# Attention tiles of a hybrid decoder layer: tail sums ahead of the fox logits, the fox V column as a unit of its own tile, TensorE's tiles unrolled

## The reference, cut to the token mixer

```python
def stick_breaking_block(q_blk, k_pre, v_pre, q_start):
    z = einsum('bhqd,bhkd->bhqk', q_blk, k_pre) * HEAD_DIM ** -0.5
    causal = s_idx < t_idx
    log_1m_beta = where(causal, log_sigmoid(-z), 0.0)
    tail = cumsum(log_1m_beta, axis=3, reverse=True) - log_1m_beta
    a = where(causal, exp(log_sigmoid(z) + tail), 0.0)
    return einsum('bhqk,bhkd->bhqd', a, v_pre)

def forgetting_block(q_blk, k_pre, v_pre, fcum_q, fcum_k, q_start):
    logits = einsum('bhqd,bhkd->bhqk', q_blk, k_pre) * HEAD_DIM ** -0.5
    logits = logits + fcum_q[..., :, None] - fcum_k[..., None, :]
    logits = where(s_idx <= t_idx, logits, -inf)
    return einsum('bhqk,bhkd->bhqd', softmax(logits, axis=-1), v_pre)

def token_mixer(h, w_in, b_forget, sb_group_g, fox_group_g, w_out):
    proj = h @ w_in        # q_sb k_sb v_sb q_fx k_fx v_fx (512 columns each), 8 forget logits
    fcum = cumsum(log_sigmoid(f_logit + b_forget))
    merged = concat(rms_norm(o_sb, sb_group_g), rms_norm(o_fx, fox_group_g))
    return merged @ w_out
```

## Time and profile before

| | us |
|---|---|
| three runs: median (lowest to highest) | 1053.41 (1053.15 to 1053.46) |
| the profiled execution's own time | 1053.56 |
| its span, first to last instruction | 1051.7 |
| mixer, PE's first product to the end of the last tile | 358.6 to 599.3 of the span |

### The profile page before, as it was taken

One profiled execution on the slowest core, in us unless ns is written; L12 is line 12 of the kernel. 1 busy time (PEld: TensorE's weight loads), 2 busy tenths in 40 slices (PEclk: granted clock), 3 DMA queues, 4 the chain that ended last, 5 costly groups with the idle time before them and its releaser, 6 DMA issues.

```text
span 1051.7 us, 16615 instructions
## 1 busy us (share of the span) xinstructions
PE 1038.6 (99%) x6118; PEld 923.7 (88%) x6118; DVE 785.5 (75%) x1107; ACT 558.4 (53%) x922; POOL 10.0 (1%) x33
## 2 busy tenths in 40 slices
PE   9999999999999999999999999999999999999997
PEld 7889999998888878888888888889999998888886
DVE  6889888864343789796969889899888865454655
ACT  6634444343333558686869846544444344344645
POOL 1000000000002000000000000000000000000000
PEclk9999999999999999999999999999999999999999
DMA  6353423303323233232312122263423305444002
GB/s 213 94 175 106 135 81 106 98 21 111 95 94 100 61 100 90 62 88 58 85 51 61 56 85 81 83 188 108 134 81 105 97 21 162 144 135 159 1 21 80
DMA packets 99948, 100.59 MB, mean 96 GB/s; under 512 B 6672, under 2 KB 82192, under 8 KB 99888
## 3 DMA queue, kind: packets, MB, share of 16 engines
q1 hardware_dynamic: 99472, 99.47, 31.2%
q10 hardware_dynamic: 416, 0.30, 0.1%
HBM read 94.44 MB, written 2.10 MB: 92 GB/s over the span
## 4 chain that ended last, share of the span: by engine, by line
PE 87%; DVE 6%; ACT 4%; issue 2%; DMA 0%; DVEq 0%; ACTq 0%
PE bank L1758 27%; PE bank L1759 27%; PE bank L1760 27%; PE bank L2100 2%; DVE w_r L1110 1%; PE bank L2115 1%; DVE scratch L1656 1%; ACT scratch L847 0%; DVE big L1436 0%; DVE big L1453 0%; PE bank L2064 0%; ACT scratch L845 0%; DVE big L1433 0%; DMA gains<-in_gains 0%; DVE acc L1130 0%
## 5 line engine op out<-in xcount | busy, mean ns | idle before, releaser
L1110 DVE TENSOR_TENSOR w_r<-w_raw,w_r 128x512 fp32r<-128x512 f32 x204 | 138.0, 688 | 134.2 <-ACT w_r L611 128.6
L1758 PE MATMUL bank<-big,w_r 128*128 128x512 f32 (+1 forms) x676 | 236.1, 349 | 0.1
L1759 PE MATMUL bank<-big,w_r 128*128 128x512 f32 (+1 forms) x676 | 235.1, 348 | 0.0
L1760 PE MATMUL bank<-big,w_r 128*128 128x512 f32 (+1 forms) x676 | 235.0, 348 | 0.0
L611 ACT ACTIVATE w_r<-w_raw 128x512 fp32r<-128x512 f32 x204 | 125.3, 627 | 182.4 <-PE bank L1760 179.1
L1758 PE MATMUL bank<-big,xg 128*128 128x256 f32 (+1 forms) x728 | 214.2, 294 | 0.0
L1760 PE MATMUL bank<-big,xg 128*128 128x256 f32 (+1 forms) x728 | 213.7, 294 | 0.0
L1759 PE MATMUL bank<-big,xg 128*128 128x256 f32 (+1 forms) x728 | 213.7, 293 | 0.0
L666 ACT ACTIVATE xg<-over 128x1024 fp32r<-128x1024 f32 x72 | 75.4, 1055 | 143.4 <-DVE over L1199 90.0
L1758 PE MATMUL bank<-xg,w_r 128*128 128x512 f32 x378 | 150.1, 397 | 0.6 <-DVE scratch L1427 0.6
L1759 PE MATMUL bank<-xg,w_r 128*128 128x512 f32 x378 | 147.4, 390 | 0.0
(11 more groups left out here) (204 smaller groups left out, 1270.1 us busy)
## 6 DMA issues: line engine op xcount, KB each, us to landing
w_raw<-in_ffn_w_down SPq DMA_DIRECT2D x88, 256.0 KB, 2.7
over<-in_ffn_w_gate SPq DMA_DIRECT2D x24, 512.0 KB, 4.1
over<-in_ffn_w_up SPq DMA_DIRECT2D x24, 512.0 KB, 5.4
w_raw<-in_w_in SPq DMA_DIRECT2D x36, 256.0 KB, 3.1
w_raw<-in_ffn_w_up SPq DMA_DIRECT2D x24, 256.0 KB, 2.8
w_raw<-in_ffn_w_gate SPq DMA_DIRECT2D x23, 256.0 KB, 2.8
w_raw<-in_ffn_w_up SPq DMA_DIRECT2D x8, 512.0 KB, 5.8
w_raw<-in_ffn_w_gate SPq DMA_DIRECT2D x8, 512.0 KB, 6.8
```

What stands on the lines that cost most here:

```text
L1110: dve.tensor_tensor(w_slot(1, slot, 0, 4 * P), w_raw[:, slot, :], plain(w_slot(0, slot, 0, 4 * P)), SUB).then_inc(w_lo, 1)
L1758: pe.matmul(dst, w_hi_ap, m_hi, start=start, stop=False, skip_group_check=True)
L1759: pe.matmul(dst, w_lo_ap, m_hi, start=False, stop=False, skip_group_check=True)
L1760: return pe.matmul(dst, w_hi_ap, m_lo, start=False, stop=stop, skip_group_check=True)
```

## The change

- On PE the tail sums come ahead of the fox logits in every head: `project(0)`, in the first head the transpose of the sb V, the tail sums, `first_logits`, in the first head the transpose of the fox V, `project(1)`, `logits(1)`, and then as before. In the last tile the parts stand where they stood between these, parts(0) ahead of the tail sums.
- On ACT and DVE the softmax of logits 3, 2, 0 comes behind the sb weights, directly ahead of that of logits 1, and the split of the fox V behind both. `weigh(0)` waits as before, the first head's for both V splits.
- `mixer_start` projects five column groups in ten units, sb V in two units of its own (`mix_v`). Fox V is projected by `project(0)` of the tile itself; the other five of a tile are still projected one tile ahead, in the order fox q, fox k, sb q, sb k, sb V. The last tile gets one projection (24 matmuls), in its first head. The number of matmuls stays as it was.
- `qk_split(j + 1, 0)` (sb q and k), which follows logits 1 of the second head, now waits for that head's `project_out(1)`; the fox one waits for a column of the first head.
- The forget gate's matmuls are spread over the chunks; its weights are split at the first chunk, and unit splits between chunks begin at the second chunk; DVE's gate chain stands ahead of the hold of q and k.
- SP's order follows the units; `double_k` and `double_fx` of the last tile stand two parts earlier.
- PE's tiles are unrolled; ACT and DVE keep their loops.

The diff, cut to its core, with eight columns of indentation taken off:

```diff
 U_MIX = U_DOWN[0] + DOWN_UNITS
+U_TILE = U_MIX + TILE_UNITS - 2
...
+MIX_PAIRS = [(3, 4), (0, 1)]
+MIX_FIRST = [(2, 0), (2, 1), None, (3, 0), (3, 1), (0, 1), (0, 0), (1, 1), (1, 0), None]
+MIX_V = [u for u, unit in enumerate(MIX_FIRST) if unit is None]
+MIX_BANK = [0, 1, 7, 4, 6]
+TILE_COLS = [[5, 3, 4], [0, 1, 2]]
...
     w_six = w_in[:, :, 0:6 * 512].rearrange("p k (c n) -> p k c n", n=512)
-    for j, (kp, cp) in enumerate(MIX_FIRST):
+    for j, unit in enumerate(MIX_FIRST):
         u = U_MIX + j
+        if unit is None:
+            kh = 1 - MIX_V.index(j)
+            load_unit(u, u % SLOTS, w_in[:, 4 * kh:4 * kh + 4, 512 * 2:512 * 2 + P], 4)
+            continue
+        kp, cp = unit
...
-    for tile in range(1, TILES):
+    def tile_unit(tile, j):
+        c = TILE_COLS[j // 6][j % 6 // 2]
+        kh = j % 2
+        at = 512 * c + (tile if c == 5 else tile + 1) * P
+        u = U_TILE + TILE_UNITS * tile + j
+        load_unit(u, u % SLOTS, w_in[:, 4 * kh:4 * kh + 4, at:at + P], 4)
+    for tile in range(TILES - 1):
         for j in range(TILE_UNITS):
-            c, kh = divmod(j, 2)
             if j == 5:
-                double_k(tile - 1)
-            if j == (6 if tile == 1 else 5):
-                double_fx(tile - 1)
-            load_unit(U_MIX + TILE_UNITS * tile + j, j % SLOTS,
-                      w_in[:, 4 * kh:4 * kh + 4, 512 * c + tile * P:512 * c + tile * P + P], 4)
+                double_k(tile)
+            if j == (5 if tile else 6):
+                double_fx(tile)
+            tile_unit(tile, j)
+    tile_unit(TILES - 1, 0)
+    tile_unit(TILES - 1, 1)
     w_out = t["w_out"][0].rearrange("(k p) n -> p k n", p=P)
     for r in range(PARTS):
-        if r == 5:
+        if r == 3:
             double_k(TILES - 1)
             double_fx(TILES - 1)
...
         first = isinstance(tile, int) and tile == 0
-        act.wait_ge(hold_ready, (2, 4)[kind] if first else 6 * tile + 3 * kind)
+        act.wait_ge(hold_ready, (2, 4)[kind] if first else 6 * tile + (3, 1)[kind])
...
     def mixer_start():
-        for j in range(EARLY, 9):
-            ahead(U_MIX, 0, TILE_UNITS, j)
...
-        ahead(U_MIX, 0, TILE_UNITS, 9)
         qk_split(0, 1)
...
             if hh == 0:
                 v_split(j, 0)
-                v_split(j, 1)
                 if not more:
+                    ahead(U_TILE, j, TILE_UNITS, 0)
+                    ahead(U_TILE, j, TILE_UNITS, 1)
                     unit(0)
-            for i, b in enumerate((3, 2, 0)):
-                softmax_exp(i, b)
             if hh == 1 and more:
                 unit(0)
                 unit(1)
...
                 act.activation(el[:, c], Z[b][:, 0:Z_W[b]], ACT.Exp).then_inc(a_exp, 1)
                 act.wait_ge(a_exp, 3 * hd + b + 2)
                 act.activation(sp_r[0][:, c], el[:, c], ACT.Copy).then_inc(a_hi, 1)
+            for i, b in enumerate((3, 2, 0)):
...
             softmax_exp(3, 1)
+            if hh == 0:
+                v_split(j, 1)
             if hh == 0 and more:
...
+    def beside_x(k):
+        if k == 0:
+            act.wait_ge(wf_zero, 1)
+            act.wait_ge(wf_loaded, 16)
+            act.activation(wf_part[0], wf_raw, ACT.Copy).then_inc(wf_hi, 1)
+        else:
+            ahead(U_MIX, 0, TILE_UNITS, k - 1)
...
+    def beside_x(k):
+        if k == 0:
+            dve.wait_ge(wf_hi, 1)
+            dve.tensor_tensor(wf_part[1], wf_raw, plain(wf_part[0]), SUB).then_inc(wf_lo, 1)
+        else:
+            ahead(U_MIX, 0, TILE_UNITS, k - 1)
...
-        for j in range(EARLY, 9):
-            ahead(U_MIX, 0, TILE_UNITS, j)
-            if j == EARLY:
-                dve.wait_ge(wf_hi, 1)
-                dve.tensor_tensor(wf_part[1], wf_raw, plain(wf_part[0]), SUB).then_inc(wf_lo, 1)
+        ahead(U_MIX, 0, TILE_UNITS, 7)
         dve.memset(scan_ones, 1.0).then_inc(f_step, 1)
-        dve.wait_ge(rms_ready, SUM_AT[N_MIX_PRE] + 1)
-        dve.memset(acc[:, 0, :], 0.0).then_inc(acc_zero, 1)
-        dve.memset(acc[:, 1, :], 0.0).then_inc(acc_zero, 1)
         def hold_pair(cp):
             dve.wait_ge(w_used, U_MIX + MIX_FIRST.index((ORDER[1][-1] // 2, cp)) + 1)
             for c in MIX_PAIRS[cp]:
-                hold_tile_column(c, bank[MIX_BANK[c]][:, :], first_v if c in (2, 5) else hold_ready)
-        hold_pair(2)
+                hold_tile_column(c, bank[MIX_BANK[c]][:, :])
         dve.wait_ge(f_done, 1)
         dve.tensor_copy(fl, bank[3][32:32 + HEADS, :]).then_inc(f_half, 1)
         dve.wait_ge(f_half, 1)
         dve.tensor_tensor(fz, bank[3][0:HEADS, :], fl, ADD).then_inc(f_half, 1)
         dve.wait_ge(f_half, 2)
+        dve.wait_ge(rms_ready, SUM_AT[N_MIX_PRE] + 1)
         dve.tensor_tensor(fz, fz, rms[0:HEADS, 0, :], MUL).then_inc(f4_ready, 1)
+        hold_pair(1)
         dve.sem_inc(o_added, 1)
...
         dve.tensor_tensor(f4[32:32 + HEADS, :], fl, plain(f4[0:HEADS, :]), SUB).then_inc(f_step, 1)
         qk_split(0, 1)
-        hold_pair(1)
+        dve.wait_ge(w_used, U_MIX + MIX_V[1] + 1)
+        hold_tile_column(2, bank[MIX_BANK[2]][:, :], first_v)
         for b in range(3):
             softplus(0, b)
         softplus_lo(0)
-        ahead(U_MIX, 0, TILE_UNITS, 10)
-        ahead(U_MIX, 0, TILE_UNITS, 11)
+        ahead(U_MIX, 0, TILE_UNITS, 8)
+        ahead(U_MIX, 0, TILE_UNITS, 9)
+        dve.memset(acc[:, 0, :], 0.0).then_inc(acc_zero, 1)
+        dve.memset(acc[:, 1, :], 0.0).then_inc(acc_zero, 1)
...
+                if more or (hh, g) == (0, 0):
+                    dve.wait_ge(w_used, U_TILE + 6 * hh + 2 * g + 2 + TILE_UNITS * j)
+                    hold_tile_column(TILE_COLS[hh][g], G_BANK[:, :])
             def softmax_max(b):
                 lb, at, w = L_AT[b]
                 dve.reduce_max(stat[:, 0, b:b + 1], L_BANKS[lb % 2][:, at:at + w], AX, negate=True).then_inc(neg_max, 1)
             project_out(0)
-            dve.wait_ge(l_done, 3 * hd + 1)
-            softmax_max(3)
-            dve.wait_ge(l_done, 3 * hd + 2)
-            softmax_max(2)
-            softmax_max(0)
             def normalise(i, b):
                 lb, at, w = L_AT[b]
...
                 dve.tensor_scalar(pr[:, c], pr[:, c], stat[:, 2, b:b + 1], None, MUL).then_inc(p_scaled, 1)
             if hh == 0:
                 v_split(j, 0)
-                v_split(j, 1)
                 if not more:
+                    ahead(U_TILE, j, TILE_UNITS, 0)
+                    ahead(U_TILE, j, TILE_UNITS, 1)
                     unit(0)
-            for i, b in enumerate((3, 2, 0)):
-                normalise(i, b)
             if hh == 1 and more:
                 unit(0)
                 unit(1)
-            dve.wait_ge(l_done, 3 * hd + 3)
-            softmax_max(1)
             for b in range(3):
                 c = slice(512 * b, 512 * b + Z_W[b])
                 dve.wait_ge(a_hi, 3 * hd + b + 1)
                 dve.tensor_tensor(sp_r[1][:, c], el[:, c], plain(sp_r[0][:, c]), SUB).then_inc(a_lo, 1)
+            dve.wait_ge(l_done, 3 * hd + 1)
+            softmax_max(3)
+            dve.wait_ge(l_done, 3 * hd + 2)
+            softmax_max(2)
+            softmax_max(0)
+            for i, b in enumerate((3, 2, 0)):
+                normalise(i, b)
+            dve.wait_ge(l_done, 3 * hd + 3)
+            softmax_max(1)
             normalise(3, 1)
+            if hh == 0:
...
+            pe.wait_ge(xg_lo, x_at(1, i))
+            start(2)
+            last = blocks(bank[MIX_BANK[2]][:, :], (U_MIX + j) % SLOTS, P * kk,
+                          xg[:, 0, k, :], xg[:, 1, k, :], i == 0, i == DC - 1)
+            if kk == 3:
+                last.then_inc(w_used, 1)
+        def f_gate(chunks):
+            for k in chunks:
+                pe.wait_ge(xg_lo, x_at(1, ORDER[1].index(k)))
+                for part in range(2):
+                    last = pe.matmul(bank[3][:, :], wf_cols[:, k, :], xg[:, part, k, :],
+                                     start=k == ORDER[1][0] and part == 0, stop=k == ORDER[1][-1] and part == 1,
+                                     skip_group_check=True)
+            return last
         for kk in range(2):
-            for j in range(3):
-                mix(j, kk)
-        for j in range(3, TILE_UNITS):
-            mix(j, 0)
-            mix(j, 1)
-            if j == 7:
-                sum_rows(N_MIX_PRE, bank[2])
-            if j == 8:
-                pe.wait_ge(xg_lo, x_at(1, DC - 1))
-                pe.wait_ge(wf_lo, 1)
-                for k in range(DC):
-                    for part in range(2):
-                        last = pe.matmul(bank[3][:, :], wf_cols[:, k, :], xg[:, part, k, :], start=k == 0 and part == 0,
-                                         stop=k == DC - 1 and part == 1, skip_group_check=True)
-                last.then_inc(f_done, 1)
+            mix(0, kk)
+            mix_v(2, kk)
+            mix(1, kk)
+        for kk in range(2):
+            mix_v(2, 2 + kk)
+            mix(3, kk)
```

(74 more changed lines are left out.)

35 lines of the change are left out of this document (16 added, 19 removed).

## The result

| | before | after |
|---|---|---|
| median of four runs, us (lowest to highest) | 1053.43 (1053.15 to 1053.48) | 1093.63 (1092.98 to 1094.10) |
| the profiled execution's own time | 1053.56 | 1094.10 |
| its span | 1051.7 | 1092.2 |

The change makes the kernel slower: the ratio is 1.0379, with a 95% interval of 1.0366 to 1.0392. The prediction was 1092.0.

The account below looks back on a forecast made before the run. It took PE as the bound, busy 1038.6 of 1051.7 us, its chains covered by projections. From 1053.56, 2.1 + 16.0 + 4.1 + 9.7 + 4.8 + 2.0 = 38.7 gave 1092 us, range 1076 to 1099.

Parts of the forecast that it names:

- Start: Mixer start: chunk waits and a later chain to the softplus put tile 0's tail sums at 409.0 against 406.83, +2.1.
- The wait of 3.8 us: PE's wait in tile 0, listed with 3.65 and 4.05 in the last tile; clock falls behind all three, +4.8.
- First heads: Tiles 0 to 2: `weigh(0)` waits 2.5 us for the fox V split behind the softmax; head 28.9 against 26.1.
- Clock behind `weigh(0)`: Tiles 0 to 2: slow clock behind the three `weigh(0)` waits, from nothing to 4.8, taken as +2.0.
- Second heads: Tiles 0 to 2: DVE's next-tile work queues behind the late softmax, softplus at 22.4; head 29.5 against 27.3.
- Ahead of the last tile: parts(0) waits 2.0 us for the hold in its bank, then takes 2.06 ahead of the tail sums: +4.1.
- Last tile: `logits(1)` waits 3.65 and 4.05 for the exponential, second head's sums another 1.0; 42.8 against 33.1, +9.7.
- Predicted tail sums of the last tile at 592: Sign to look for in the profile after: the last tile's tail sums start at 592.
- these sums would be slow again: Last tile's tail sums: slow before and after the change, so no difference was counted for them.
- Unrolling: PE's tile borders: the gap ends with DVE's hold, not the branch; between nothing and -0.9 us, taken as nothing.
- The most there was to win: PE's standing or slow time at tile borders and mixer ends: some 7 us is all a new order could win.

Follow-up runs that it names:

- `late_unit_split`: The changed kernel with ACT's and DVE's mixer unit splits begun one chunk later, at the third chunk of x: 1089.16 us, ratio 1.0337 to the kernel before.
- `last_parts_first`: The changed kernel with parts(1) of the last tile ahead of logits(1) in both heads: 1086.93 us, ratio 1.0322 to the kernel before.
- `v_split_early`: The changed kernel with the fox V split on ACT and DVE ahead of the softmax of logits(1) in first heads: 1086.47 us, ratio 1.0317 to the kernel before.
- `sb_columns_first`: The changed kernel with columns projected in the order fox V, sb q, sb k, fox q, fox k, sb V: 1091.33 us, ratio 1.0361 to the kernel before.
- `hold_first_in_the_changed_kernel`: The changed kernel with DVE holding project_out(2) ahead of a unit's low part in second heads of tiles 0 to 2: 1093.88 us, second heads 29.52.
- `unroll_only`: The kernel before with PE's tiles unrolled and nothing else: 1053.91 us against 1053.70 in the same rounds, ratio 1.0003.
- `hold_first`: The kernel before with DVE holding project_out(2) ahead of a unit's low part in second heads: 1052.59 us against 1053.70 in the same rounds, ratio 0.9988.
- `v_transposes_thrice`: The kernel before with the last tile's V transposes done three times over, giving PE work in its 2.33 us wait: 1053.99 us, ratio 1.0003.

## Why the prediction was right, step by step

The profiled execution grew by 40.54 us where the sum said 38.7. Starts of after are taken less 0.68 us, by which PE's first product came later (359.29 for 358.61). In the mixer, counted so, 2.8 (start) + 24.3 (from there to the last tile's sums) + 12.5 (last tile) = 39.6 us are found. With the 0.68 that is 40.3; the last 0.2 lies outside and isn't named.

- **Start: predicted +2.1, and 1.6 of clock; measured +2.8** (410.29 - 0.68 = 409.61 for 406.83), and nothing for the clock. The cause is settled by `late_unit_split`: the extra unit split. Chunk waits were 0.40, 0.82 and 1.52. The clock term was mis-sized: the clock did fall behind the scores, but `project(0)`, which it slowed, lies under the softplus, for which PE then still waited 2.37 us. In `last_parts_first` the fall at this place lasted longer and that wait was 1.12, yet the sums came 50.95 us after PE's first product for 51.00 here. The sums ran at full clock. The wait of 3.8 us that the prediction names here is worked out nowhere in it; there were two, 3.11 for k's copy and 2.37.
- **First heads: predicted 28.9; measured 29.18** where the clock held. The mechanism is shown by `v_split_early`.
- **Clock behind `weigh(0)`: predicted 2.0; measured 3.2.** Two of three falls, 1.6 us each (30.77 and 30.83 less 29.18). This term can't be foreseen from the wait: the clock fell behind the same 2.42 us in tiles 0 and 1 here, in tile 1 alone in `last_parts_first` (29.18, 30.77, 29.17) and in no tile in `sb_columns_first`.
- **Second heads: predicted 29.5; measured 29.5.** The stations at 17.1, 22.9 (the hold's end, 464.00 less 441.06) and 22.4 all hold; the transposes waited 0.41 for the 0.6 and `project(0)` 1.18 for the 1.35. The softplus chain sets it, as `hold_first_in_the_changed_kernel` shows. `sb_columns_first` gives 0.57 of the 2.2 to the column order. That the remaining 1.6 is the late softmax of `logits(1)` in front of DVE's queue was walked through and not tried by itself.
- **Ahead of the last tile: predicted +4.1; measured 33.76 - 29.52 = 4.24**, the hold behind softplus, output and addition. It is read from the rows, not tried: the wait of 2.37, which the profile leaves unnamed, plus 2.16 of parts(0), less the 0.28 that the other second heads wait ahead of their sums.
- **Last tile: predicted 42.8 and 3.2 of clock, 46.0; measured 639.53 - 593.86 = 45.67.** Waits 3.34, 3.90 and 0.73 for the 3.65, 4.05 and 1.0 of the prediction. That the sum is so near is luck in part. Its 42.8 carried over the 1.6 us of slow sums from before, and they didn't come. The clock cost more than 3.2: 2.7 in the first head (25.58 for the 22.84 of `late_unit_split`, which had no fall there) and 1.55 in the second (628.03 to 633.77, 5.74 us, for 4.19 before). `last_parts_first` shows the cover: one order of two calls takes 3.4 us off the first of the two heads.
- **Predicted tail sums of the last tile at 592; measured 593.86**, which is the 0.68 and 2.0 more from the first heads (0.28 each and 1.2 of clock), less the 0.9 that the start came below its 2.1 + 1.6. The prediction's remark that these sums would be slow again was wrong: they took 2.70. In this execution no fall followed the wait; in `late_unit_split` one did, and it slowed parts(0), which stands between the wait and the sums, and not the sums.
- **Unrolling: nothing, and shown** by `unroll_only`. The Trainium skill ("Runtime: NRT & Kernel Launch", "Instruction fetch mechanics") says that a taken branch whose target lies outside the fetched pages stalls the engine, and prefers unrolling for it; no run here shows such a stall. The measurement decides: unrolling won nothing, and `hold_first` shows the wait that filled the border.
- **The most there was to win** (some 7 us) was put too high: filling its 2.33 us and speeding up the slow sums gave nothing that the runs can tell (0.3 us in the trace), the border gave 1.1. The 1.0 us ahead of the tail sums of tile 0 was not tried.

The mechanism, the place and the size hold. The clock's terms are near in sum and not one by one: 1.6 too much in tile 0, 1.2 too little behind `weigh(0)`, 1.1 too little in the last tile, and 1.6 of slow sums that stayed away. That these cancel is luck.

## What to carry to other kernels

A chain on the element-wise engines costs nothing while a projection stands behind the product that starts it, and its full length once the projection is moved ahead of that product. Price a reordering by walking from the moved product to the next thing that needs its result, with every split queued behind it on that engine. And before you count a wait as a gain, look at what is late next: filling one or shortening slow matmuls wins only what the following chain lets through. Count the clock behind a wait of 2 to 3 us as a chance and not as a price: here it fell in some executions and not in others.

## What was not expected of the hardware

- The same idle time of PE, 2.42 us, was followed by a granted clock of 0.50 in two of three heads and of 1.00 in the third; a fall there cost 1.6 us. The 2.33 us ahead of the last tile's sums were followed by 0.50 in the kernel before and by 1.00 in `unroll_only` and `hold_first`. The wide range of some runs fits this (`hold_first_in_the_changed_kernel`: 1096.87 us at a mean granted clock of 0.986, the other three 1091.72 to 1093.92 at 0.989), but only one execution of each kernel has a trace.
- Matmuls at half clock cost little where another engine's chain is later anyway: 4.29 us for the sums of the last tile before, 2.93 in `v_transposes_thrice`, and the next tail sums 0.3 us earlier.
- An idle time listed as "issue" can still be a wait for a semaphore: the 2.37 us at 591.70 come to an end 0.1 us after the hold on DVE (590.91 and 0.69), for which the program has parts(0) wait.
